# Which 64-token tile of a product-key expert layer shares the reading of V, and how its full-width weights are formed

## The reference, cut to what matters

```python
qry = (xi @ w_query).reshape(PEER_BLOCK, PEER_HEADS, 2, PEER_HALF)
s = jnp.einsum('thpc,pnc->thpn', qry, sub_keys)
s1, i1 = lax.top_k(s[:, :, 0], PEER_TOPK)
s2, i2 = lax.top_k(s[:, :, 1], PEER_TOPK)
cand = (s1[..., :, None] + s2[..., None, :]).reshape(PEER_BLOCK, PEER_HEADS, PEER_TOPK * PEER_TOPK)
cidx = (i1[..., :, None] * PEER_KEYS + i2[..., None, :]).reshape(...)
top_s, pos = lax.top_k(cand, PEER_TOPK)
idx = jnp.take_along_axis(cidx, pos, axis=-1)
gate = jax.nn.softmax(top_s, axis=-1)
hid = jax.nn.gelu(jnp.einsum('td,thkd->thk', xi, expert_u[idx]), approximate=False)
return jnp.einsum('thk,thkd->td', gate * hid, expert_v[idx])
```

## Time and profile before

| What | us |
|---|---|
| median of 3 runs (lowest, highest) | 4403.11 (4401.84, 4405.47) |
| the profiled execution | 4408.51 |
| its span | 4406.7 |
| PE busy in it | 3442.7 |
| DVE busy in it | 2870.2 |
| POOL busy in it | 1468.2 |
| ACT busy in it | 641.5 |

### The profile page before, as it was taken

One profiled execution on the slowest core, in us unless ns is written; L12 is line 12 of the kernel. 1 busy time (PEld: TensorE's weight loads), 2 busy tenths in 40 slices (PEclk: granted clock), 3 DMA queues, 4 the chain that ended last, 5 costly groups with the idle time before them and its releaser, 6 DMA issues. The chain is left out here.

```text
span 4406.7 us, 41392 instructions
## 1 busy us (share of the span) xinstructions
PE 3442.7 (78%) x14727; PEld 2479.1 (56%) x14727; DVE 2870.2 (65%) x4685; ACT 641.5 (15%) x1596; POOL 1468.2 (33%) x1096
## 2 busy tenths in 40 slices
PE   6999999988589998998778942213899975799950
PEld 5888888877466766776556632203444444444420
DVE  2333333304778887887844859999855579855577
ACT  2222222201123223332200110000000001000000
POOL 1001001001444343443531435674332222422265
PEclk9999999999789999999789975555799975699985
DMA  6766666487789999999986529999999998899998
GB/s 174 226 206 205 201 190 205 137 300 239 256 342 365 364 359 348 368 367 343 348 334 257 209 95 376 383 405 325 353 421 421 422 374 290 329 421 421 422 421 332
DMA packets 426692, 1383.33 MB, mean 314 GB/s; under 512 B 40748, under 2 KB 274912, under 8 KB 276552
## 3 DMA queue, kind: packets, MB, share of 16 engines
q0 software_dynamic: 125504, 893.81, 52.3%
q1 hardware_dynamic: 288312, 386.22, 25.8%
q10 hardware_dynamic: 12672, 100.67, 5.8%
HBM read 1250.80 MB, written 129.62 MB: 313 GB/s over the span
## 5 line engine op out<-in xcount | busy, mean ns | idle before, releaser
L1938 DVE CUSTOM_DVE_ANT_0 ex_ring<-ex_ring,ex_xi 128x2048 f32<-128x2048 f32 x544 | 1237.5, 2287 | 257.3 <-DMA ex_ring<-in_peer_u_dram,idx_all 141.2
L1890 POOL DMA_INDIRECT ex_ring<-in_peer_u_dram,idx_all x384 | 589.7, 1536 | 694.5 <-DVE ex_hid L1938 611.0
L1951 DVE SCALAR_TENSOR_TENSOR ex_y<-ex_ring,ex_wt,ex_y 128x2048 f32<-128x2048 f32 x284 | 669.6, 2358 | 182.4 <-DMA ex_ring<-in_peer_v_dram,idx_all 91.4
L870 PE MATMUL heads_b_pj<-xnT_b,lead 128*128 128x304 f32 x2048 | 594.5, 428 | 10.1 <-DVE mixT_b L1539 4.0
L2569 PE MATMUL rest_acc<-rest_hot_col,rest_hot_row 128*128 128x64 f32 x1024 | 251.7, 428 | 366.1 <-DVE rest_hot_col L2617 362.4
L2578 PE MATMUL rest_acc<-lead,rest_wide_act 128*128 128x512 f32 x1024 | 448.8, 596 | 0.9 <-ACT rest_wide_act L2537 0.9
L2569 PEld LDWEIGHTS rest_acc<-rest_hot_col,rest_hot_row 128*128 128x128 f32 x1024 | 227.9, 328 | 391.1 <-DVE rest_hot_col L2617 386.5
L2578 PE MATMUL rest_acc<-rest_v_more,rest_wide_act 128*128 128x512 f32 x1024 | 444.7, 592 | 0.0
L870 PEld LDWEIGHTS heads_b_pj<-xnT_b,lead 128*128 128x128 f32 x2048 | 370.6, 193 | 118.1 <-issue 11.8
L1890 POOL DMA_INDIRECT ex_ring<-in_peer_v_dram,ex_idx_s x160 | 246.4, 1540 | 428.7 <-DVE ex_y L1951 364.8
L2578 PEld LDWEIGHTS rest_acc<-lead,rest_wide_act 128*128 128x128 f32 x1024 | 195.8, 191 | 247.7 <-issue 246.4
(11 more groups left out here) (607 smaller groups left out, 4392.3 us busy)
## 6 DMA issues: line engine op xcount, KB each, us to landing
lead<-w_scratch SPq DMA_DIRECT2D x64, 1024.0 KB
lead<-in_peer_v_dram SPq DMA_DIRECT2D x64, 1024.0 KB, 9.1
rest_v_more<-in_peer_v_dram SPq DMA_DIRECT2D x64, 1024.0 KB, 9.2
heads_a_w<-in_w_in_dram SPq DMA_DIRECT2D x38, 1024.0 KB, 6.1
w_scratch<-heads_a_w ACTq DMA_DIRECT2D x38, 1024.0 KB, 4.0
lead<-in_w_in_dram SPq DMA_DIRECT2D x26, 1024.0 KB, 6.1
w_scratch<-lead ACTq DMA_DIRECT2D x26, 1024.0 KB, 4.4
out_a_w<-in_w_out_dram SPq DMA_DIRECT2D x7, 2048.0 KB, 14.1
```

The lines of the kernel that those rows point to most:

```text
L870: last = nc.tensor.matmul(pj[j % PJ][:, 0:N], slot(j)[:, k, :], xnT[:, k, :], start=(k == 0), stop=(k == KT - 1))
L1890: pool.indirect_dma_start(self.ring[:, i % RING, :], None, self.tables[which], bass.IndirectOffsetOnAxis(ap=self.index(s, g, k), axis=0)). ...
L1938: nc.vector.tensor_tensor_reduce(ring, ring, self.tokens(s)[:], 1.0, 0.0, ALU.mult, ALU.add, self.hid[:, g % 2, k:k + 1]).then_inc(self.se ...
L1951: nc.vector.scalar_tensor_tensor(y, ring, wt, y, ALU.mult, ALU.add).then_inc(self.sem["consumed"], 1)
```

## The change

The set of FIRST's whole tile (128 tokens) no longer shares the reading of V; its V is gathered (eight turns). The two sets of 64 tokens with two heads at once, one of FIRST and one mixed of both groups, make up tile 1 of the dense product together: the first has columns 0 to 63 of the weights, the other 64 to 127 (`column`). Tile 0 is LATER's first tile. There are 288 items of V as before.

The quads are formed once, 64 in place of 128, with all 128 columns of each. A quad of tile 1 takes two tokens of each 64-token set (they lie in the same partitions' halves for two heads), with two products of 64 partitions accumulated. ACT copies half of the columns into `wide_act`, the other half into `later`, a part of the constants' tile that is no longer needed, from which SP writes it to DRAM (`wide_scratch`); it is read back over the used half in two parts, when PE has used 32 and 64 pieces. PE takes all 128 pieces of V in one run, without copying a sum out between. V's pieces from the fifth on are issued behind the last save. `wide_act` has the column innermost, so a weight load reads values 32 apart. `OVERLAP` goes to 14 + 290 + 44 + 8 + 28 = 384 items.

```diff
-OVERLAP = {"norm": 14, "heads": 266, "out": 24, "ffn": 4, "route": 12}
+OVERLAP = {"norm": 14, "heads": 290, "out": 44, "ffn": 8, "route": 28}
...
-            (FIRST, [prompt_part(0, FIRST, 1)], HEADS, False, 0),
-            (FIRST, [split(r, FIRST, 0, slice(T0, T0 + half)) for r in range(2)], HEADS // 2, False, None),
+            (FIRST, [prompt_part(0, FIRST, 1)], HEADS, False, None, 0),
+            (FIRST, [split(r, FIRST, 0, slice(T0, T0 + half)) for r in range(2)], HEADS // 2, False, 1, 0),
...
-            (LATER, [prompt_part(0, LATER, 0)], HEADS, False, 1),
+            (LATER, [prompt_part(0, LATER, 0)], HEADS, False, 0, 0),
             (LATER, [split(r, *p) for r in range(2) for p in ((FIRST, 0, slice(T0 + half, P)), (LATER, 2, slice(0, LATER.rows[2])))],
-             HEADS // 2, True, None),
-            (LATER, [prompt_part(0, LATER, 1)], HEADS, False, None),
+             HEADS // 2, True, 1, P // 2),
+            (LATER, [prompt_part(0, LATER, 1)], HEADS, False, None, 0),
...
     def quad_mark(n):
 
-        half, d, t = quad_of(n)
-        q = t // QUAD
-        if half == 0:
-            return start + 3 * q + 0.2 if d == 0 else ready + q + 0.2
-        return ready + QUADS + AGAIN + d * QUADS + q + 0.2
-
-    def out_mark(half):
-        return quad_mark(2 * QUADS) + 8 if half == 0 else stream.items - 8
+        d, q = n // QUADS, n % QUADS
+        return ready[d] + (0.5 if d else 1.8) * q + 0.2
+
+    out_mark = stream.items - 8
...
-        wide_act, v_more = sb("wide_act", [P, 2, CHALF, P]), sb("v_more", [P, PLACES - 2, D])
-        hot_row, hot_col = sb("hot_row", [P, 2, QUAD, KEYS]), sb("hot_col", [P, 2, QUAD, CHALF])
+        wide_act, v_more = sb("wide_act", [P, 2, 2, P, CQUARTER]), sb("v_more", [P, PLACES - 2, D])
+        hot_row, hot_col = sb("hot_row", [P, 2, QUAD, KEYS]), sb("hot_col", [P, 2, QUAD, KEYS])
...
+            for c in range(PLACES):
+                load(c)
+            for pair in range(QUADS):
+                d, q = 2 * pair // QUADS, 2 * pair % QUADS
+                sp.wait_ge(sem["kept"], 2 * pair + 2)
+                for a in range(2):
...
+                    sp.dma_start(place, source).then_inc(sem[f"saved{pair % 2}"], 16)
+            for c in range(PLACES, KEYS):
+                load(c)
+                for a in range(2):
+                    if c == (a + 1) * CQUARTER + PLACES - 1:
...
+                            sp.wait_ge(sem["used"], (a + 1) * CQUARTER)
+                            sp.dma_start(wide_act[:, d, a], scr["wide"][a, d]
+                                         ).then_inc(sem[f"again{a}"], 16)
...
+                        on = slice(j // 2 * (P // 2), (j // 2 + 1) * (P // 2))
+                        at = (n % 2 * 2 + j // 2) * BANK + j % 2 * KEYS
+                        out = acc[:, d, at:at + KEYS]
+                        for r in range(2):
+                            last = nc.tensor.matmul(out, hot_row[on, n % 2, 2 * r + j % 2, :], hot_col[on, n % 2, 2 * r + j % 2, :],
+                                                    start=(r == 0), stop=(r == 1))
+                    last.then_inc(sem["built"], 1)
+            pe.wait_ge(sem["kept"], 2 * QUADS)
+            for n in range(KEYS):
+                quarter, c = n // CQUARTER, n % CQUARTER
+                if quarter >= 2 and c == 0:
+                    pe.wait_ge(sem[f"again{quarter - 2}"], 32)
+                pe.wait_ge(sem[f"v_in{n % PLACES}"], 16 * (n // PLACES + 1))
                 for d in range(2):
...
+                    for b in range(0, D, BANK):
+                        last = nc.tensor.matmul(acc[:, d, b:b + BANK], weights(d, quarter, c), v_place(n)[:, b:b + BANK],
+                                                start=(n == 0), stop=(n == KEYS - 1))
+                last.then_inc(sem["used"], 1)
```

More of the change, by code:

```diff
@@ L1711, with __init__ @@
     class Set:
-        def __init__(self, group, parts, groups, first, at, second, dense):
+        def __init__(self, group, parts, groups, first, at, second, dense, column):
             self.group, self.parts, self.groups, self.first, self.at = group, parts, groups, first, at
-            self.end, self.whole, self.second, self.dense = first + groups, len(parts) == 1, second, dense
+            self.end, self.whole, self.second, self.dense, self.column = first + groups, len(parts) == 1, second, dense, column
     def __init__(self, nc, ctx, ins, outs, mem, scr):
@@ L1814, in sums_before @@
     def sums_before(self, s):
-        return next((r for r in reversed(self.sets[:self.sets.index(s)]) if r.second == s.second and r.dense is None), None)
+        return next((r for r in reversed(self.sets[:self.sets.index(s)]) if r.dense is None), None)
     def last_u(self, s):
@@ L2489, in v_place, with weights, apart, load @@
             return lead.rows[:, n % PLACES, :] if n % PLACES < 2 else v_more[:, n % PLACES - 2, :]
+        def weights(d, quarter, c):
+            return wide_act[:, d, quarter % 2, :, c]
+        def apart(place):
+            return place.rearrange("p a (s u) c -> p a s u c", s=2)
         @block.sync
         def _(sp):
-            stream.spread(sp, LATER)
-            for c in range(KEYS):
+            def load(c):
                 if c >= PLACES:
@@ L2499, in _ @@
         @block.gpsimd
         def _(pool):
[L2502 to L2513, removed]
@@ L2515, in _ @@
-            Marks(gathers(), dense_sums()).run()
+            stream.gather(pool, start, out_mark)
+            pool.wait_ge(sem["staged"], 1)
+            alone(pool, sem["passed"])
+            pool.dma_start(whole.parts[0].y_rows, sums[:, 0, :], accum_op=ALU.add).then_inc(sem["dense_out"], 16)
+            for part, low in [(prompt.parts[0], 0), (mixed.parts[0], P // 2), (mixed.parts[1], P // 2)]:
+                pool.dma_start(part.y_rows, sums[low + part.on.start:low + part.on.stop, 1, :], accum_op=ALU.add
+                               ).then_inc(sem["dense_out"], 16)
@@ L2516, in _ @@
+            stream.gather(pool, start, stream.items)
             pool.wait_ge(stream.sem["y_out"], 16 * stream.y_outs)
@@ L2552, in _ @@
         def _(pe):
-            for half in range(2):
-                for d in range(2):
[L2555 to L2580, removed]
@@ new lines, in _ @@
+            for d in range(2):
+                pe.wait_ge(sem["coded"], d + 1)
+                for i, source in enumerate((code[:, 0, :], code[:, 1, :], stream.wide_wt[d][:])):
+                    last = nc.tensor.transpose(acc[:, d, i * P:(i + 1) * P], source, cst("ident"))
+                last.then_inc(sem["turned"], 1)
+                for q in range(QUADS):
+                    n = d * QUADS + q
+                    pe.wait_ge(sem["hot_ready"], n + 1)
+                    if q >= (2 if d else 4):
+                        pe.wait_ge(sem["kept"], n - (1 if d else 3))
+                    for j in range(QUAD):
+                        if d == 0:
+                            out = acc[:, d, n % 4 * BANK + j * KEYS:n % 4 * BANK + (j + 1) * KEYS]
+                            last = nc.tensor.matmul(out, hot_row[:, n % 2, j, :], hot_col[:, n % 2, j, :], start=True, stop=True)
+                            continue
+                        on = slice(j // 2 * (P // 2), (j // 2 + 1) * (P // 2))
[5 more added lines that the diff above has]
+                    last.then_inc(sem["built"], 1)
@@ L2604, in quads @@
             def quads():
[L2605 to L2606 removed]
+                for n in range(2 * QUADS):
+                    d, q = n // QUADS, n % QUADS
                     yield quad_mark(n)
[L2608 removed]
+                    if q == 0:
                         dve.wait_ge(sem["codes"], d + 1)
```

124 lines of the change are left out of this document (75 added, 49 removed).

## The result

The changed kernel took 4285.88 us (median of 4 runs, 4276.91 to 4292.42), beside 4404.29 for the kernel before beside it (4401.84 to 4411.33). The ratio is 0.9727, with a 95% interval of 0.9706 to 0.9748: 118 us less, where 96 were forecast. The profiled execution took 4285.55 us, of which 4283.8 are the span.

A forecast was written before the change was run, and what follows sets the result against it. No engine bounds it throughout: PE fills dense stretches, DVE the buildings, gathers run between. The rest -163 and the front +67 make -96 us, from the median 4403 to 4307 us; range 4240 to 4405.

The forecast's parts named there:

- the rest: Rest of the experts, first item to end: 1601 us against 1764, 163 us less, with bounds of 90 and 190.
- What bounds it: No engine throughout; in the rest of the experts PE fills dense stretches, DVE fills buildings, gathers alone take 2.49 us an item.
- Gathers to the first quad: Start of the rest: 132 items of U at 2.49 us, 329, plus 10 for four V places: 339 us.
- First building: First 32 quads, one per 1.8 items, DVE deciding at 1.7 us a quad: 182 us.
- Second building: 32 quads of the mixed tile, two per item: 110 us, bounds 90 (DVE) and 167 (PE at 1.2 GHz).
- Rival 3: Second building runs at 1.2 GHz throughout: 57 us more, 4364 us; chance 0.15.
- Dense stretch: PE's dense products in one run: 884 us as before plus 10 for two reloads, 894 us.
- The end: After the dense products: 8 held items' 55 us plus 5 for the copies, 60 us.
- The front: 64 more items before the rest: heads 25, mixing 5, ffn 9, routing 28; sum 67 us, bounds 18 and 153.
- Rival 2: Heads, mixing, ffn and routing take each added item whole: 153 us on against 163 off, 4393 us; chance 0.15.
- The strided load: Dense weight loads read values 32 apart: up to 0.43 us a load is hidden under the product, all above isn't.
- rival 1: Strided weight load outlasts the dense product, from 0.43 us a load: 4600 us at three times the present load; chance 0.12.

The follow-up runs named there:

- b_once: Kernel before, its second half multiplying with weights left from the first, the second building of quads left out (wrong sums): 4341.96 us, ratio 0.9852.
- a_quota324: Changed kernel with OVERLAP 14 + 266 + 24 + 4 + 16 = 324, so 60 additional early items run in the rest again: 4359.72 us, ratio 0.9882.
- a_fullrows: Changed kernel with the second building's products over all 128 partitions in place of 64 at a time (wrong weights for the mixed tile): 4285.2 us, one execution.
- a_contig: Changed kernel with dense weight loads reading 128 neighbouring values in place of values 32 apart (wrong sums): 4285.73 us, ratio 0.9722.
- a_narrow: Changed kernel with dense products 256 columns wide in place of 512, strided loads kept, twice as many records: 4312.85 us, one execution.
- a_heads310: Changed kernel with OVERLAP 14 + 310 + 44 + 4 + 12 = 384, routing's 16 and ffn's 4 additional items moved to heads: 4275.38 us, ratio 0.9698.

## Why the prediction was right, step by step

The forecast was 4307 us, the time 4285.88, inside the range, and by the mechanism as put, but for the price of PE's records in the second building. The terms of the rest added up to 26 us too many. (The bounds of 90 and 190 for the rest are rough: the terms named with them add up to less than 84 and to 199. Nothing here hangs on them.)

- **What bounds it.** It held: the dense product at full clock, DVE in the buildings, gathers between them. b_once and a_quota324 show two parts of the gain, each by itself: 67 us for forming once on the kernel before, 74 for the items moved on the changed one. They don't add up to the 124: what the change gives without the 60 items is 50, forming once together with its costs (wider columns, saves, reloads), and no run parts these.
- **Gathers to the first quad**: 339 forecast, 346 measured (2708.6 to 3054.8). **First building**: 182, measured 181 (DVE 180.14 of 181.00, granted 0.50), so 1.7 us a quad held: on DVE a quad of the second building takes 3255.06 - 3253.43 = 1.63.
- **Second building**: 110, measured 91. This is the term that carries the miss. I priced PE's record at 0.16 us at nearly full clock and doubled it for 1.2 GHz. But the 32 records of two quads took 3.18 us in the fastest batch (0.10 each, granted 1.00) and 5.13 in the slowest (0.16 each, granted 0.50). Two things were wrong in my price: it had been read from short batches, as the last section shows, and from products of 128 rows. So PE never outlasted DVE, and the bound that stood in the sum for DVE, 90, was the value to take. Rival 3 (1.2 GHz throughout, 57 us more) fell in its condition, since the clock was 0.67, and in its price: even the slowest batch takes 5.13 us of the 5.47 that DVE needs for two quads and an item, so by these batches it would have cost nothing. The Trainium skill, TensorE: Matmul & The Clock Gate, on packing small matmuls, says that a weight load overlaps a running matmul when its row group differs; by it the stretch would stand at DVE's 90. The stretch came out so, and the trace agrees in the price: at 1.2 GHz a record is 0.16 us with alternating halves of rows and 0.21 without. That the time of a_fullrows is the same doesn't speak against the rule, since there PE was granted 1.00.
- **Dense stretch**: 894, measured 887. The two reloads cost 5 us, not 10. 226 instructions of DVE on ex_ring stand in it, the 234 less 8 that were forecast.
- **The end**: 60, measured 54, with 10 instructions of DVE left.
- **The front**: 67, measured 66, but by errors that cancel, which is luck. Heads 25, measured 17 (2229.8 to 2246.8) between these two executions. Mixing 5, measured 0: DVE took 42 us more in the same 172 us, from its waits for PE. ffn 9, measured 10. Routing 28, measured 39: 16 items, 2.4 us each, whole. DVE was busy 42 us more there, and what it idles went only from 28 us to 24: the gaps of before weren't used. Why not is argued, not shown: its own small operations depend on each other. Rival 2 (front gives all back) fell in heads and mixing and held in ffn and routing.
- **The strided load** (rival 1): 297 ns and under cover, by a_contig without effect on the time. The Trainium skill, SBUF — State Buffer, says under the DMA port swizzle that each access to a new line of 16 bytes pays a penalty. The trace agrees that there is one, 106 ns on a load of 128 values, less than a nanosecond each; it is far from what rival 1 needed, which was over 0.43 us a load. With half the cover (a_narrow) it came to some 24 to 27 us.
- **Sum**: the rest -189 where -163 were forecast. Of the 26 us, 19 are the second building, 7 the dense stretch and 6 the end, less 7 for the gathers ahead of them; what is left is rounding.

What stays open: mixing's first product, which ends heads, begins at 2219, 2221 and 2230 us in a_quota324, b_once and the kernel before (266 items), and at 2242 to 2248 in the five traces with 290. The 24 items cost 17 us between before and after, but 12 to 29 between other pairs, 22 by the means (0.9 each), so my 25 was nearer than the 17 makes it look. Part of the 10 us that a_heads310 gains may be such chance too. No run here shows where these differences come from.

## What to carry to other kernels

Where a background stream of fixed work runs under every stage, removing a stage is worth only its excess over the stream's pace; after it, ask how many items of the stream are left when the main engine ends, and move these to the stage where the engine that they use waits (here mixing, at 0 us each), before those where it is full (2.4 us each). Price a building stretch by its fullest engine. Price a weight load or a short matmul by the distance of its records in a long batch without gaps: the duration of one includes what overlaps with the next, and busy time over count of short batches includes their starts and ends. A layout that made a weight load slower was free here, with products twice as long as the load's pace.

## What the hardware showed beside this

**The granted clock.** In the second building of after PE was busy 64.5 of 80 us with products of 64 rows and was granted 0.68 on average; in the same 80 us of a_fullrows it was busy 56.8 us with as many products of 128 rows and was granted 1.00 throughout. Six other runs with the products of 64 rows had 0.68 or 0.69 in 80 us of the same stretch (PE busy 63.5 to 64.9); the one with 128 rows is a single execution. The first building, products of 128 rows with PE busy 67 of 181 us, had 0.50. In after the batches of two quads went back and forth between the two levels (the chain of waits, columns as above):

```profile
3320.99 5.13 PE rest_acc L2600 x32
...
3331.94 3.18 PE rest_acc L2600 x32
```

The first of them was granted 0.50 (1.2 GHz) and the second 1.00 (2.4 GHz). It cost nothing here, since DVE sets the pace at both levels. Why the two kernels were granted different clocks no run tells.

**Short batches hide the price of a record.** In the first building 8 records of 128 rows at 1.2 GHz are a batch of their own, 2.07 us, 0.26 each; in a_fullrows such records followed each other at the same clock at 0.21. In routing 8 records at 2.4 GHz are 1.44 us, 0.18 each, where 32 of them in a_fullrows are 3.84, 0.12 each. The timelines, of after and of the kernel before:

```profile
3102.09 2.07 PE L2594 MATMUL rest_acc<-rest_hot_col,rest_hot_row 128*128 128x128 f32 x8 [3.81 <-DVE rest_hot_col L2663]
```

```profile
2451.45 1.44 PE L2257 MATMUL route_b_ps<-skT,route_b_q 128*128 128x128 f32 x8
```

So a price read from short batches is too high, by a quarter at 1.2 GHz and by half at 2.4. Half the rows in alternation bring a quarter at 1.2 GHz (0.16 against 0.21), and less at 2.4 (0.10 against 0.12).

**A strided weight load.** 128 values 32 elements apart take 297 to 309 ns where neighbours take 190, but one can begin every 0.22 us, since loads overlap. Neighbours can at least every 0.12: that is the distance of a_fullrows' records at 2.4 GHz, each with a load of its own.
